# Inverse by level products in an RWKV recurrence: one direction's products cross to the other half of the partitions, and two chunks share each mask, copy and turn

## The reference, cut to what matters

```python
for d in range(2):                                   # forward and backward in time
    flip = flip_time if d == 1 else identity
    yc, s_ctx = wkv7_scan(zero_state, *rwkv7_dir_inputs(cx, d, flip))    # 256 context tokens
    yl, _ = wkv7_scan(s_ctx, *rwkv7_dir_inputs(lat, d, flip))            # 512 latent tokens
    y_lat = y_lat + flip(yl)
# rwkv7_dir_inputs gives r, exp(log_w[d]), kk, a[d], k_dir[d], v for 16 heads of 64 features
```

## Time and profile before

| | us |
|---|---|
| median of three executions | 3018.33 (3014.95 to 3025.99) |
| profiled execution | 3016.63 |
| its span, first to last instruction | 3015.0 |
| stretch of the 24 quads | about 305 to 990 |

### The profile page before, as it was taken

One profiled execution on the slowest core, in us unless ns is written; L12 is line 12 of the kernel. 1 busy time (PEld: TensorE's weight loads), 2 busy tenths in 40 slices (PEclk: granted clock), 3 DMA queues, 4 the chain that ended last, 5 costly groups with the idle time before them and its releaser, 6 DMA issues. The chain is left out here.

```text
span 3015.0 us, 63742 instructions
## 1 busy us (share of the span) xinstructions
PE 2835.5 (94%) x27233; PEld 2335.6 (77%) x27233; DVE 1866.0 (62%) x3013; ACT 1418.8 (47%) x2195; POOL 453.6 (15%) x434
## 2 busy tenths in 40 slices
PE   7899999998999899999989999999989999999999
PEld 3795677777778668887649999999975756678877
DVE  4852565556665357765678888888866157466652
ACT  1212555655555342221237777777754346243331
POOL 1003345556543110000001000000010010000000
PEclk8999999999999999999999999999999999999999
DMA  5454000000000276654329999999962210222222
GB/s 211 161 209 145 31 22 21 22 21 13 12 3 3 85 251 253 273 210 188 136 111 392 383 363 372 365 372 367 368 233 79 94 60 22 97 84 85 97 105 77
DMA packets 73846, 482.17 MB, mean 160 GB/s; under 512 B 11107, under 2 KB 13027, under 8 KB 32144
## 3 DMA queue, kind: packets, MB, share of 16 engines
q1 hardware_dynamic: 59360, 418.48, 36.7%
q0 software_dynamic: 11952, 51.91, 4.6%
q10 hardware_dynamic: 2304, 8.39, 0.7%
HBM read 457.20 MB, written 34.13 MB: 163 GB/s over the span
## 5 line engine op out<-in xcount | busy, mean ns | idle before, releaser
L2412 DVE TENSOR_TENSOR sb_moe_w_lo<-w_ring,sb_moe_w_hi 128x1408 fp32r<-128x1408 f32 (+1 forms) x132 | 255.2, 1934 | 69.6 <-ACT sb_moe_w_hi L2357 67.5
L2260 PE MATMUL ps<-sb_moe_w_hi,sb_x_feat_lo 128*128 128x352 f32 x832 | 273.5, 329 | 5.0 <-DVE sb_moe_w_lo L2412 4.9
L2262 PE MATMUL ps<-sb_moe_w_hi,sb_x_feat_hi 128*128 128x352 f32 x832 | 267.5, 322 | 0.0
L2261 PE MATMUL ps<-sb_moe_w_lo,sb_x_feat_hi 128*128 128x352 f32 x832 | 266.9, 321 | 0.0
L2357 ACT ACTIVATE sb_moe_w_hi<-w_ring 128x2816 fp32r<-128x2816 f32 x80 | 204.3, 2553 | 3.2 <-DMA w_ring<-w_moe_up 2.5
L2260 PE MATMUL ps<-sb_moe_w_hi,sb_hid_feat_lo 128*128 128x256 f32 x572 | 163.2, 285 | 4.0 <-DVE sb_hid_feat_lo L2543 4.0
L2260 PEld LDWEIGHTS ps<-sb_moe_w_hi,sb_x_feat_lo 128*128 128x128 f32 x832 | 156.1, 188 | 11.6 <-issue 10.8
L2262 PE MATMUL ps<-sb_moe_w_hi,sb_hid_feat_hi 128*128 128x256 f32 x572 | 161.8, 283 | 0.0
L2261 PE MATMUL ps<-sb_moe_w_lo,sb_hid_feat_hi 128*128 128x256 f32 x572 | 161.8, 283 | 0.0
L2261 PEld LDWEIGHTS ps<-sb_moe_w_lo,sb_x_feat_hi 128*128 128x128 f32 x832 | 157.0, 189 | 0.0
L1439 PE MATMUL ps<-sb_tb,w_ring 64*64 64x64 f32 x3840 | 140.2, 219 | 16.9 <-ACT sb_tb L1604 15.6
(11 more groups left out here) (552 smaller groups left out, 7623.3 us busy)
## 6 DMA issues: line engine op xcount, KB each, us to landing
w_ring<-w_moe_up SPq DMA_DIRECT2D x67, 1408.0 KB, 8.5
sb_hm<-w_ada SPq DMA_DIRECT2D x48, 1024.0 KB, 7.0
w_ring<-w_ffn SPq DMA_DIRECT2D x22, 1024.0 KB, 4.9
w_ring<-w_up SPq DMA_DIRECT2D x22, 1024.0 KB, 4.8
sb_b_again<-w_moe_up SPq DMA_DIRECT2D x13, 1408.0 KB, 8.7
sb_hm<-w_moe_up SPq DMA_DIRECT2D x13, 1408.0 KB, 8.5
sb_t_again<-w_moe_up SPq DMA_DIRECT2D x13, 1408.0 KB, 8.0
w_ring<-w_moe_down SPq DMA_DIRECT2D x13, 1408.0 KB, 7.8
```

Source lines behind the costliest of these rows:

```text
L2260: pe.matmul(out, x_lo, w_hi, start=first, stop=False)
L2261: pe.matmul(out, x_hi, w_lo, start=False, stop=False)
L2262: return pe.matmul(out, x_hi, w_hi, start=False, stop=end)
L2412: return V.tensor_tensor(WL[:, s, w], raw[raw_at(c, i)[0]][:, w], WH[:, s, w].bitcast(F32), ALU.subtract)
```

## The change

- `X` and `T` of direction 1 cross the halves: the `X` product of direction 1 reads partitions of one head and writes the PSUM partitions of the other; the mask leaves it there; the `T` product of direction 1 takes both operands from that other half and writes back to the head's own half. Direction 0 stays where it was.
- The results go to other banks: a pair of chunks (2j, 2j+1) shares two banks, one per direction, where each chunk had its own.
- Mask, copy and turn are made once for two chunks: 128 by 256 in place of twice 128 by 128. The counters are named by the odd chunk, so `X` and `T` of either chunk wait for the pair's.
- The turned inverse of direction 1 must stand in the other half. `turn` becomes three transposes: one of 128 partitions for direction 0 of both chunks, and two of 64 partitions for direction 1, each from one half to the other. `first` becomes one transpose of 128 by 256, a wait for it, and two crossing transposes (counter `cross`), for which the first `T` waits in place of `firstT`.
- The order: a pair's `turn` comes right ahead of the pair's `X` items; before, turns were spread between single `X` and `T` items. The number of items is smaller, so features and outputs fall a little differently.

```diff
@@ -1010,7 +1010,7 @@
                 out += [(p, f"trans{n}") for n in cur[i:i + 1 - i % 2]]
                 if i in (1, 2):
                     out += [(pp, f"{'WU'[i - 1]}{n}") for n in prev[0:1]]
-            out += [(p, f"first{n}") for n in cur]
+            out += [(p, f"first{n}") for n in cur[1::2]]
             links = []
             for n in prev:
                 links += [[(pp, f"{x}{n}")] for x in "WU"] * (n % 4 > 0)
@@ -1021,10 +1021,10 @@
             for lev in range(LAST + 1):
                 for head in "XT":
                     for n in cur:
+                        if turns and head == "X" and n % 2 == 0:
+                            out.append(turns.pop(0))
                         out.append((p, f"{head}{lev}.{n}"))
-                        if turns and (head == "X" or n % 4):
-                            out.append(turns.pop(0))
-                        if head == "T" and lev < LAST:
+                        if head == "T" and lev < LAST and n % 2:
                             turns.append((p, f"turn{lev}.{n}"))
                     if links:
                         out += links.pop(0)
@@ -1085,11 +1085,13 @@
         def following(names, table):
             return [y + x[len(x.rstrip("0123456789.")):] for x in names for y in table.get(x.rstrip("0123456789."), ())]
 
+        both = [x for x in fronts if x[0] not in "XT" or int(x.split(".")[1]) % 2]
+
         pe_f = self.marks("front_pe", [x for x in fronts if x.rstrip("0123456789.") in ("score", "trans", "X", "T")])
         pe_c = self.marks("chain_pe", links)
-        act_f = self.marks("front_act", following(fronts, {"trans": ["tr"], "T": ["t"]}))
+        act_f = self.marks("front_act", following(both, {"trans": ["tr"], "T": ["t"]}))
         act_c = self.marks("chain_act", following(links, {"W": ["W"], "U": ["U"], "Y": ["Y"]}))
-        dve_f = self.marks("front_dve", following(fronts, {"score": ["LK"], "first": ["first"], "X": ["x"], "turn": ["turn"]}))
+        dve_f = self.marks("front_dve", following(both, {"score": ["LK"], "first": ["first", "cross"], "X": ["x"], "turn": ["turn"]}))
         dve_c = self.marks("chain_dve", [f"z{x[1:]}" for x in links if x[0] == "Z"])
         pool_f = self.marks("front_pool", following(fronts, {"score": ["I", "firstT"]}))
         feats = main + late
@@ -1138,6 +1140,12 @@
 
             def halves(x):
                 return x.rearrange("p (a b) -> p a b", a=2)
+
+            def level(i, to):
+                return ps[:, i - 1:i + 1, to:to + P].rearrange("p d (c n) -> p d c n", c=2)
+
+            def two(x, i):
+                return x[:, i - 1:i + 1].rearrange("p c d n -> p d c n")
 
             def turned(tokens, h):
 
@@ -1402,9 +1410,9 @@
                                 pe.wait_ge(s_re, KT)
                                 pe.wait_ge(f_pool.sem, f_pool.at("R", p))
                             if n >= 4:
-                                pe.wait_ge(act_f.sem, act_f.at(f"t{LAST}.{n - 4}", p))
+                                pe.wait_ge(act_f.sem, act_f.at(f"t{LAST}.{n - 4 | 1}", p))
                             elif p:
-                                pe.wait_ge(act_f.sem, act_f.at(f"t{LAST}.{n + 8}", p - 1))
+                                pe.wait_ge(act_f.sem, act_f.at(f"t{LAST}.{n + 8 | 1}", p - 1))
                             for d in range(2):
                                 for o, w in ((0, FB), (2, FK)):
                                     for hh in heads:
@@ -1431,24 +1439,27 @@
                                     last = pe.transpose(ps[:, 4, to:to + P], w[:, d, first:first + P], ident)
                         elif head == "X":
                             if lev:
-                                pe.wait_ge(act_f.sem, act_f.at(f"t{lev - 1}.{n}", p))
+                                pe.wait_ge(act_f.sem, act_f.at(f"t{lev - 1}.{n | 1}", p))
                             else:
-                                pe.wait_ge(dve_f.sem, dve_f.at(f"first{n}", p))
+                                pe.wait_ge(dve_f.sem, dve_f.at(f"first{n | 1}", p))
                             for d in range(2):
-                                for hh in heads:
-                                    last = pe.matmul(ps[hh, i, d * CH:(d + 1) * CH], M[hh, d, 0, :], tb[hh, d, 0, :],
+                                for h, hh in enumerate(heads):
+                                    last = pe.matmul(ps[heads[h ^ d], (i & 2) + d, (i & 1) * CH:(i & 1) * CH + CH], M[hh, d, 0, :], tb[hh, d, 0, :],
                                                      start=True, stop=True)
                         elif head == "T":
-                            pe.wait_ge(dve_f.sem, dve_f.at(f"x{lev}.{n}", p))
+                            pe.wait_ge(dve_f.sem, dve_f.at(f"x{lev}.{n | 1}", p))
                             if lev:
-                                pe.wait_ge(dve_f.sem, dve_f.at(f"turn{lev - 1}.{n}", p))
+                                pe.wait_ge(dve_f.sem, dve_f.at(f"turn{lev - 1}.{n | 1}", p))
                             else:
-                                pe.wait_ge(pool_f.sem, pool_f.at(f"firstT{n}", p))
+                                pe.wait_ge(dve_f.sem, dve_f.at(f"cross{n | 1}", p))
+                            to = 256 + (i & 1) * CH
                             for d in range(2):
-                                to = 256 + d * CH
-                                for hh in heads:
-                                    w, src = (tb[hh, d, 1, :], x2[hh, d, :]) if lev < LAST else (x2[hh, d, :], tb[hh, d, 1, :])
-                                    last = pe.matmul(ps[hh, i, to:to + CH], w, src, start=True, stop=True)
+                                for h, hh in enumerate(heads):
+                                    at_h = heads[h ^ d]
+                                    w, src = tb[at_h, d, 1, :], x2[at_h, d, :]
+                                    if lev == LAST:
+                                        w, src = src, w
+                                    last = pe.matmul(ps[hh, (i & 2) + d, to:to + CH], w, src, start=True, stop=True)
                         elif head == "W":
                             if n:
                                 pe.wait_ge(dve_c.sem, dve_c.at(f"z{n - 1}", p))
@@ -1599,10 +1610,9 @@
                                 for h, hh in enumerate(heads):
                                     last = S.activation(TR[hh, s, i + b].rearrange("p d o n -> p (d o) n"), turned(tokens, h), ACT.Copy)
                             last.then_inc(*act_f.did(f"tr{n}"))
-                        elif head == "T":
+                        elif head == "T" and n % 2:
                             act.wait_ge(pe_f.sem, pe_f.at(x, p))
-                            S.activation(TB[:, s, i, :, int(lev == LAST), :], ps[:, i, 256:384].rearrange("p (d n) -> p d n", d=2),
-                                         ACT.Copy).then_inc(*act_f.did("t" + x[1:]))
+                            S.activation(two(TB[:, s, :, :, int(lev == LAST), :], i), level(i, 256), ACT.Copy).then_inc(*act_f.did("t" + x[1:]))
                         elif head == "W":
                             act.wait_ge(pe_c.sem, pe_c.at(x, p))
                             S.activation(Ws[:, :, :].rearrange("p d n -> p (d n)"), ps[:, 5, 0:P],
@@ -1689,13 +1699,20 @@
                                             mC[:, :, ::by, :], ALU.mult).then_inc(*dve_f.did(f"LK{n}"))
                         elif head == "first":
                             dve.wait_ge(pool_f.sem, pool_f.at(f"firstT{n}", p))
-                            V.transpose(TB[:, s, i, :, 0, :], TB[:, s, i, :, 1, :]).then_inc(*dve_f.did(x))
+                            V.transpose(TB[:, s, i - 1:i + 1, :, 0, :], TB[:, s, i - 1:i + 1, :, 1, :]).then_inc(*dve_f.did(x))
+                            dve.wait_ge(dve_f.sem, dve_f.at(x, p))
+                            for h, hh in enumerate(heads):
+                                last = V.transpose(TB[heads[1 - h], s, i - 1:i + 1, 1, 1, :], TB[hh, s, i - 1:i + 1, 1, 0, :])
+                            last.then_inc(*dve_f.did(f"cross{n}"))
                         elif head == "turn":
                             dve.wait_ge(act_f.sem, act_f.at(f"t{lev}.{n}", p))
-                            V.transpose(TB[:, s, i, :, 1, :], TB[:, s, i, :, 0, :]).then_inc(*dve_f.did(x))
-                        elif head == "X":
+                            V.transpose(TB[:, s, i - 1:i + 1, 0, 1, :], TB[:, s, i - 1:i + 1, 0, 0, :])
+                            for h, hh in enumerate(heads):
+                                last = V.transpose(TB[heads[1 - h], s, i - 1:i + 1, 1, 1, :], TB[hh, s, i - 1:i + 1, 1, 0, :])
+                            last.then_inc(*dve_f.did(x))
+                        elif head == "X" and n % 2:
                             dve.wait_ge(pe_f.sem, pe_f.at(x, p))
-                            V.tensor_tensor(Xs[:, i], ps[:, i, 0:P].rearrange("p (d n) -> p d n", d=2), mL[:, lev + 1, :, :],
```

(1 more changed line is left out.)

## The result

The changed kernel takes 3067.28 us (median of four, 3062.51 to 3073.61) where the one before, on the same chip, takes 3017.73: ratio 1.017, 95% interval 1.0147 to 1.0192: slower by 1.7%. The profiled execution took 3062.51 us, the fastest of the four; its span is 3060.9 against 3015.0, 45.9 more. The difference lies in the stage of the quads: from the first `X` to the last `T` it takes 725.2 us against 677.0, 48.2 more. `X` is now line 1447, `T` 1462, the mask 1715, the turn 1709 (direction 0) and 1711 (the two crossings), the copy 1615.

A forecast was written before the change was run, and what follows sets the result against it. PE was taken to bound each pair's first and third quads, DVE the second. A middle pair's -4.2, +1.0, -4.5 and fronts +2.1 give -5.6; six pairs -34, first -9, last -7: -50 us, 2968 us, range 2935 to 3075.

The forecast's parts named there:

- The two terms of the sum: Per quad, PE's products of `X` and `T` give back 4.7 us and DVE's masks and turns cost 1.8 us more.
- the rate: `X` and `T` on PE: an item of four chunks takes 0.47 us in place of 0.94, saving 4.7 us a quad.
- The sign beside it: In the changed profile, the busy time of the lines of `X` and `T` is near half of before.
- the term that failed: DVE's masks and turns in the levels: +1.8 us per quad, between -0.2 and +2.4.
- The lower end of this term: DVE's instructions all as close as now: 5.6 + 10 x 0.31 against 3.8 + 20 x 0.25, -0.2 us per quad.
- DVE reaches 15.9 of 18, no bound yet: First quad's levels: DVE busy 14.1 + 1.8 = 15.9 of 18 us, so the quad gains 4.2 us.
- The third quad: Its levels, PE-bound: -4.7 us from PE and +0.2 from coarser waits, together -4.5, leaving 15.9 us.
- Coarser waits: `T` waits for the mask of both chunks, the mask for both `X`: 0.5 us on first quad, 0.2 on third.
- Fronts: The stretch before each quad's levels, with `firstT` and crossings: +0.7 us each, from 0 to 1.2; +2.1 per pair of heads.
- ACT and what lies behind the stage: ACT's copies fall from 5.5 to 3.8 us per quad, off the path; the stage's whole difference reaches the end.
- The rival without overlap: Crossed products don't run beside diagonal ones of their half; `X` and `T` keep 0.94 us: +44, 3062 us; chance 0.27.
- the rival that DVE eats the gain: Products overlap in items of 0.55 us, but DVE is at its upper end and queued: 3005 to 3025 us; chance 0.13.

The follow-up runs named there:

- the uncrossed turn: The changed kernel with crossed products kept, but turn and transposes behind `first` made as if nothing crossed (direction 1's result not usable): 2992.27 us, ratio 0.9905.
- pairs only: The changed kernel with nothing crossing: banks, masks, copies and turns still shared by two chunks, a turn one 128 by 256 transpose: 3032.1 us, ratio 1.0029.

## Why the prediction was wrong

Put together (us; the ratios to before are 1.003 and 1.017 in the first row, 0.991 and 1.017 in the second):

| | turn in one transpose | three transposes |
|---|---|---|
| products in their half | 3032.1 | 3073.3 |
| products crossed | 2992.3 | 3067.3 |

With the cheap turn crossed products bring 40 us; with the three transposes 6 (1 by the ratios), less than the intervals tell apart. The turn costs 41 where PE is still slow, 75 where it is fast (42 and 80 by the ratios). The two terms of the sum can't be added, as the prediction did.

What else stands in DVE's queue in the second quad, before the change (the same quad of the next pair of heads, where DVE is busy 16.32 us):

```profile
L1643 DVE RECIPROCAL sb_kk<-sb_kk 128x128 f32<-128x128 f32 x4 | 3.7, 927 | 0.0
L1659 DVE RECIPROCAL sb_ysum<-sb_ysum 128x128 f32<-128x128 f32 x4 | 3.6, 915 | 0.0
L1704 DVE TENSOR_TENSOR sb_Z<-ps,sb_pend 128x128 f32<-128x128 f32 x4 | 1.0, 260 | 0.5 <-PE ps L1481 0.5
L1646 DVE SCALAR_TENSOR_TENSOR sb_kk<-sb_kk,sb_kq 128x768 f32<-128x768 f32 x1 | 1.0, 1004 | 0.0
L1656 DVE TENSOR_TENSOR sb_ysum<-sb_ysum,ps 128x512 f32<-128x512 f32 x1 | 0.7, 679 | 0.0
```

The prediction's steps, one by one:

- **PE: the rate right, one sign not.** `X` of four chunks is 0.69 us as 32 records, in the range that it named; less the last one's 0.22 the rate is 0.47. The sign beside it, the busy time of the lines near half of before, did not come: `X` has 103.7 us against 140.2, `T` (all levels but the last) 88.5 against 114.1. The last record of each run stays as long as it was, and stretches of lower clock are in it. The rule of the Trainium skill that spoke against it ("TensorE: Matmul & The Clock Gate", The mechanism: a weight load overlaps only with matmuls of another row group) does not hold for these products: by the prediction's estimate 32 records one after the other would take up to 1.8 us, and here they start within 0.47 with their loads, nearly four at a time, so that each row half has a crossed and a diagonal product at once. "TensorEngine Tiling (Array Packing)", Key Properties, has it right for this form.
- **DVE: the term that failed.** Forecast was +1.8 us per quad. The durations came out as forecast at the upper end (crossings 0.306, masks 0.418), and the turn at 0.92 to 0.97 us, near what was written. But a busy time is not a queue: before, the transposes, masks and reciprocals of the second quad overlapped at their ends; held ones don't. DVE's busy time there rose from 16.33 to 21.77, by 5.4 us, and the quad went from 18.4 to 23.3 in place of 19.4. Against the uncrossed turn, 0.61 us for each of eight turns is 4.9, and the quad is 5.4 us longer. The price was at hand: the prediction's own 0.9 us for a turn and 0.31 for a mask give 8 x 0.9 + 10 x 0.31 = 10.3 us of queue, and with the 10.0 us of the lines above 20.3 where its sum has 18.1. Some 0.7 of the remainder is the one `SCALAR_TENSOR_TENSOR`, which takes 1.73 us after the change and 1.00 before; why is open. The lower end of this term was also added up wrongly: 5.6 + 3.1 against 3.8 + 5.0 is -0.1, not -0.2, and with the mask's spacing of 0.175 that the same paragraph reads it is 3.8 + 3.5 before, so +1.4.
- **"DVE reaches 15.9 of 18, no bound yet": wrong in the first quad.** DVE is busy 17.35 of 23.67, not full, yet `T` waits 4.3 us for masks behind turns and scans. With a turn in one piece of 0.92 us or more, an engine at three quarters of its time here already holds up a loop with two groups. Forecast -4.2, measured +1.5. The third quad, without scans and reciprocals, has -2.1 where -4.5 was forecast.
- **Coarser waits: too cheap.** 0.7 us per pair of heads was put down; pairs only is 14 us longer over the stage than before, 1.4 per middle pair, although DVE has less to do in it.
- **Fronts:** forecast +2.1 per pair, measured 7.26, 10.15 and 9.47 against 8.47, 8.05 and 9.42, so +0.9: too dear.
- **ACT and what lies behind the stage: right.** The copies are no wait more than before (15.1 us, 15.6 before), and the stage's difference (48.2) is the span's (45.9) to 2.3 us.

The rival without overlap gave 3062 us, near the result, but by chance: its mechanism is refuted by the 0.69 us. The right mechanism was the rival that DVE eats the gain, with a price (3005 to 3025) 42 to 62 us too low. The Trainium skill's rule in "VectorE: DVE Perf Modes", Two Vector instructions with no wait between them, was weighed only for 0.6 us per quad; the trace agrees with it (two crossings 0.32 us apart in the median, where each takes 0.306, against 0.23 for a start in the same partitions).

What stays open: how much of the crossing's price is the hold and how much the doubled number of instructions (the estimate above has them about equal); an order of work in which the turn doesn't stand right ahead of its pair's mask, which no run tried; and a form in which `T` crosses and `X` doesn't, with the matrix held in both halves, which needs no crossing transpose and was not tried.

## What to carry to other kernels

Price a longer piece in an in-order queue by what stands behind it, from start to start, not by the busy share it adds. Over 192 turns, 0.48 us more for each (92 us) cost 41 us of time beside a slow PE, and 0.61 (117 us) cost 75 beside a fast one. Before halving the work of one engine, run the kernel with that work halved and the new helper's work left out. Here that kernel is 28 us faster than the one before, and this is the most that the helper may cost; it cost 75. Moving the helper to the idler engine brought nothing, since its items too stand in a loop.

## Hardware behaviour that was not expected

- 64 by 64 products in all four combinations of input and output half run together, with the two that write the same half in different banks: 32 records in 0.69 us against 1.10 with two combinations.
- A transpose of 64 partitions takes as long on DVE as one of 128 with as many elements per partition (0.306 and 0.295 us), so moving halves apart doubles the cost. ACT's copy of 64 by 128 took 0.308 us; its copies of 128 by 128, which read PSUM, took 0.277.
- A DVE instruction that begins in other partitions than its predecessor starts at the predecessor's end (0.31 to 0.32 us after its start) in place of 0.22 to 0.23.
- The granted clock is 0.84 in a quad with PE busy 15.7 of 23.3 us, and 0.94 over the stage. With the turn made cheap it is 0.99 over the stage, though one quad there has 1.00 with PE busy 12.9 of 17.9 us.
